# Attention of a decoder layer: a new order of query tiles, and VectorE's counts placed between single operations

## The reference, cut to what matters

```
dots  = einsum('bqhd,bsd->bqhs', qi, kidx) * IDX_DIM ** -0.5      # 8 indexer heads of 64
score = einsum('bqhs,bqh->bqs', relu(dots), wi)
score = where(kpos <= qpos, score, -inf)
idx   = top_k(score, 256)
s     = q . k[idx] * HEAD_DIM ** -0.5                              # 8 heads, 4 K/V heads
o     = softmax(s) @ v[idx]
```

## Time and profile before

| | us |
|---|---|
| median of 3 runs | 3550.71 (3544.14 to 3551.95) |
| the profiled execution | 3548.39 |
| its span | 3546.6 |
| outside the span | 1.8 |
| attention phase, of the span | 925.6 to 2008.6 |

### The profile page before, as it was taken

One profiled execution on the slowest core, in us unless ns is written; L12 is line 12 of the kernel. 1 busy time (PEld: TensorE's weight loads), 2 busy tenths in 40 slices (PEclk: granted clock), 3 DMA queues, 4 the chain that ended last, 5 costly groups with the idle time before them and its releaser, 6 DMA issues. The chain is left out here.

```text
span 3546.6 us, 45686 instructions
## 1 busy us (share of the span) xinstructions
PE 2941.8 (83%) x15200; PEld 1827.0 (52%) x15201; DVE 1971.5 (56%) x2856; ACT 1053.8 (30%) x1832; POOL 837.6 (24%) x1259
## 2 busy tenths in 40 slices
PE   7999999998666566666667686999999499999989
PEld 6877899988523333333445453445444333333333
DVE  2697025990267777778876367743323543444437
ACT  1111121211266675758585441000000011111113
POOL 2344333322253342414030131012120000000013
PEclk9999999999767887887879897999999599999989
DMA  3323222434100000000000265223331378677537
GB/s 120 97 92 122 90 71 75 142 120 131 46 19 13 15 13 10 10 10 7 7 7 10 81 209 185 84 101 126 118 128 39 143 274 299 261 286 286 185 132 241
DMA packets 218484, 390.29 MB, mean 110 GB/s; under 512 B 28180, under 2 KB 147220, under 8 KB 205514
## 3 DMA queue, kind: packets, MB, share of 16 engines
q1 hardware_dynamic: 184818, 268.60, 22.3%
q0 software_dynamic: 25152, 89.03, 7.5%
q10 hardware_dynamic: 8352, 30.51, 2.2%
HBM read 501.30 MB, written 88.52 MB: 166 GB/s over the span
## 5 line engine op out<-in xcount | busy, mean ns | idle before, releaser
L347 PE MATMUL p_ps_acc<-p_x_hi,p_w_hi 128*128 128x352 f32 (+2 forms) x1480 | 525.1, 355 | 26.0 <-POOL p_w_lo L284 22.3
L347 PE MATMUL p_ps_acc<-p_x_lo,p_w_hi 128*128 128x352 f32 (+2 forms) x1480 | 524.3, 354 | 0.0
L347 PE MATMUL p_ps_acc<-p_x_hi,p_w_lo 128*128 128x352 f32 (+2 forms) x1480 | 523.9, 354 | 0.0
L832 PE MATMUL q_ps_s<-a_keys,q_q_st 64*128 64x512 f32 (+3 forms) x640 | 196.5, 736 | 237.8 <-ACT q_relu L914 132.4
L532 DVE SCALAR_TENSOR_TENSOR p_conv<-p_uh,p_taps,p_conv 128x1024 f32<-128x1024 f32 x240 | 384.2, 1601 | 8.5
L2457 PE MATMUL e_ps_G<-l_wgu,e_xT 128*64 x768 | 341.8, 598 | 21.3 <-DVE e_gu_b L2574 10.8
L2459 PE MATMUL e_ps_G<-e_gu_b,e_xT 128*64 128x512 f32 x768 | 341.9, 599 | 0.0
L347 PEld LDWEIGHTS p_ps_acc<-p_x_hi,p_w_hi 128*128 128x128 f32 (+1 forms) x1480 | 277.8, 188 | 55.9 <-POOL p_w_lo L284 22.8
L347 PEld LDWEIGHTS p_ps_acc<-p_x_lo,p_w_hi 128*128 128x128 f32 (+1 forms) x1480 | 279.0, 189 | 28.5
L1016 DVE TENSOR_SCALAR_CACHE_REDUCE q_junk_dve<-q_sc,q_mid 128x384 bf16<-128x384 f32 (+6 forms) x175 | 247.0, 1411 | 82.0 <-POOL q_mid L1129 79.9
L347 PEld LDWEIGHTS p_ps_acc<-p_x_hi,p_w_lo 128*128 128x128 f32 (+1 forms) x1480 | 277.9, 188 | 27.3
(11 more groups left out here) (406 smaller groups left out, 4858.4 us busy)
## 6 DMA issues: line engine op xcount, KB each, us to landing
l_wgu<-in_w_gate_dram SPq DMA_DIRECT2D x96, 1024.0 KB
l_wgu<-in_w_up_dram SPq DMA_DIRECT2D x96, 1024.0 KB
l_wd<-in_w_down_dram SPq DMA_DIRECT2D x96, 1024.0 KB
p_w<-in_w_in_dram SPq DMA_DIRECT2D x72, 512.0 KB, 3.8
yb<-e_y SPq DMA_DIRECT2D x48, 512.0 KB, 4.6
x_gates<-featT SPq DMA_DIRECT2D x64, 256.0 KB
featT<-p_stage ACTq DMA_DIRECT2D x28, 528.0 KB
featT<-p_stage ACTq DMA_DIRECT2D x28, 512.0 KB
```

What stands on the lines that cost most here:

```text
L347: m = nc.tensor.matmul(acc[slot][tb][0:rows, 0:width], wp[:, slot, k, 0:rows], xp[:, k, at], start=(k == 0 and i == 0), stop=(k == KD - 1 ...
L832: m = nc.tensor.matmul(ps_s[x][:, k0:k1], q_st[rows, t % 2, g % 4, :], kT[rows, g % 4 // 2, a + k0:a + k1], start=True, stop=True)
```

## The change

There are two edits. The first is a table `TILES` that says which tile is done at which position: positions 0 to 15 hold tiles 0, 1, 4, 5, 10, 11, 14, 15, 12, 13, 8, 9, 6, 7, 2, 3. Everything that depended on the tile's number as a length, a row of the inputs and outputs, or the end of an accumulation now goes through `TILES`; buffers, semaphores and slots go by position as before. In blocks of keys, the three jobs of each cycle are:

| cycle | attention before | search before | dots before | attention after | search after | dots after |
|---|---|---|---|---|---|---|
| 0 | 1, 2 | 3, 4 | 5, 6 | 1, 2 | 5, 6 | 11, 12 |
| 1 | 3, 4 | 5, 6 | 7, 8 | 5, 6 | 11, 12 | 15, 16 |
| 2 | 5, 6 | 7, 8 | 9, 10 | 11, 12 | 15, 16 | 13, 14 |
| 3 | 7, 8 | 9, 10 | 11, 12 | 15, 16 | 13, 14 | 9, 10 |
| 4 | 9, 10 | 11, 12 | 13, 14 | 13, 14 | 9, 10 | 7, 8 |
| 5 | 11, 12 | 13, 14 | 15, 16 | 9, 10 | 7, 8 | 3, 4 |
| 6 | 13, 14 | 15, 16 | - | 7, 8 | 3, 4 | - |
| 7 | 15, 16 | - | - | 3, 4 | - | - |

The prologue makes the dots of 5 and 6 blocks instead of 3 and 4.

The second edit is in VectorE's order. The two operations of the first half's `sums` are taken apart: head 0, place 2, head 1, place 3, then `normalise` where it is due, place 4.

```diff
+TILES = [0, 1, 4, 5, 10, 11, 14, 15, 12, 13, 8, 9, 6, 7, 2, 3]
+
 def length(t):
-    return (t + 1) * P
+    return blocks(t) * P
+
+def blocks(t):
+    return TILES[t] + 1
+
+def rows_at(t):
+    return slice(TILES[t] * P, TILES[t] * P + P)
...
-                sp.dma_start(qi_st[:, t % 2], c.featT[COL_QI:COL_KI, t * P:(t + 1) * P]...
+                sp.dma_start(qi_st[:, t % 2], c.featT[COL_QI:COL_KI, rows_at(t)]...
...
-                    for k in range(t + 1):
+                    for k in range(blocks(t)):
...
-                def sums(t, m, half):
+                def sums(t, m, half, heads=(0, 1)):
...
-                    for x in range(2):
-                        src, w = relu[:, n % 2, x, 0:b - a], wi_tok[:, t, 2 * m + x:2 * m + x + 1]
+                    for x in heads:
+                        src, w = relu[:, n % 2, x, 0:b - a], wi_tok[:, TILES[t], 2 * m + x:2 * m + x + 1]
...
                     behind(g, 1)
-                    if dotted_in(g):
-                        sums(dotted_in(g), g % 4, 0)
+                    if here:
+                        sums(here, g % 4, 0, (0,))
                     behind(g, 2)
+                    if here:
+                        sums(here, g % 4, 0, (1,))
+                    behind(g, 3)
                     if g % 4 == 0 and t:
                         normalise(t - 1)
-                    behind(g, 3)
                     behind(g, 4)
```

More of the change, by code:

```diff
@@ L674, in __init__ @@
             for x in range(2):
-                for a, b in cuts(t + 1, 4):
+                for a, b in cuts(blocks(t), 4):
                     self.turns[g, x, a // 4] = turn
@@ L712, in last_turn @@
     def last_turn(self, g, x):
-        return self.turns[g, x, g // 4 // 4]
+        return self.turns[g, x, TILES[g // 4] // 4]
 def attend_prompt(nc, c, kT, kiT, v_tok, wi_tok):
@@ L876, in values @@
                             m = nc.tensor.matmul(ps_o[x * HD:(x + 1) * HD, g % 4, :], v_tok[:, k, kv * HD:(kv + 1) * HD], pT[:, x, k, :],
-                                                 start=(k == 0), stop=(k == t))
-                            if k == t:
+                                                 start=(k == 0), stop=(k == TILES[t]))
+                            if k == TILES[t]:
                                 m.then_inc(pv_done, 1)
@@ L919, in keep_turned @@
                         act.wait_ge(pv_done, 2 * g)
-                    for a, b in cuts(g // 4 + 1, 4):
+                    for a, b in cuts(blocks(g // 4), 4):
                         n = at.turns[g, x, a // 4]
@@ L1010, in bracket @@
                     ch.link(nc.vector.tensor_reduce(least[:, t:t + 1], row, AX.X, ALU.min))
-                    ch.link(nc.vector.tensor_tensor(row[:, t * P:], row[:, t * P:], mk[:, P:2 * P], ALU.add))
+                    ch.link(nc.vector.tensor_tensor(row[:, length(t) - P:], row[:, length(t) - P:], mk[:, P:2 * P], ALU.add))
                     nc.vector.tensor_reduce(most[:, t:t + 1], row, AX.X, ALU.max).then_inc(range_ready, 1)
@@ L1049, in behind, with masked @@
                         choose(t + 1, n - HALVINGS - 5)
-                def masked(g, u):
+                def masked(g, u, heads=(0, 1)):
                     t = g // 4
+                    if u >= len(cuts(length(t), 1024)):
+                        return
                     a, b = cuts(length(t), 1024)[u]
@@ L1092, in _ @@
                     t, nxt = g // 4, (g + 1) // 4
-                    if g and dotted_in(g - 1):
-                        sums(dotted_in(g - 1), (g - 1) % 4, 1)
+                    last, here = (dotted_in(g - 1) if g else None), dotted_in(g)
+                    if last:
+                        sums(last, (g - 1) % 4, 1)
                         if g % 4 == 0:
-                            bracket(dotted_in(g - 1))
+                            bracket(last)
                     if g + 1 < NSLOT:
```

9 lines of the change are left out of this document (4 added, 5 removed).

## The result

The changed kernel runs in 3502.61 us (median of 4 runs, 3500.33 to 3504.78), against 3550.53 us for the kernel before (3544.14 to 3551.95). The ratio is 0.9874, with a 95% interval of 0.9861 to 0.9888.

The account below looks back on a forecast made before the run. No engine is near full over the span; VectorE's idle time, cycle by cycle in the attention phase, was to decide. Prologue +5, loop work -5, idle -8 and split -7 gave -15 us: 3536 us, range 3504 to 3566.

Parts of the forecast that it names:

- Cycle 7: Last cycle, attention of 3 and 4 blocks: 39 us in all, VectorE idle 26 us instead of 66.6, a gain of 40.
- Part 3, the idle time by cycle: VectorE's idle time over the attention phase's eight cycles: 276 us instead of 284, 8 us less.
- Cycle 3: Longest attention beside search and dots: 1.6 us a slot more than old cycle 5, so VectorE idle 48 us.
- the ring: Long cycles' chain of relu freeing a bank, TensorE's scores, VectorE's mask and ScalarE's copies; longer scores and transposes lengthen it.
- the paragraph on the clock: TensorE's clock: a denser middle would run cycle 3 at full clock and the last cycle slow; the forecast did not use it.
- Part 4, the split: VectorE's count put between the two heads' sums: 7 us less, at most 27, at least nothing.
- Part 1, the prologue: Dots before the loop, now of 5 and 6 blocks: about 3.4 us a pair of heads, loop starts 5 us later.
- Part 2, the work: VectorE's work in the loop: from 767 to 762 us, 5 us less, as dots of four blocks move to the prologue.
- signs of being wrong: In the profile after: cycle 3 over 208 us, cycles 2 and 3 each under 32 idle, or middle waits unchanged in number.
- The split pays in full: Rival: the count between the sums gains its whole bound of 27 us, 20 more than forecast, 3516 us; chance 0.17.
- Slower, by the ring of cycle 3: Rival: TensorE stays at the low clock in cycle 3, 3.8 us a slot, 30 over the cycle, 3566 us; chance 0.15.
- Idle time is a constant of 28 us a cycle: Rival: VectorE's idle time is 7 x 28.4 + 26 = 225 us, 59 less than 284, kernel 3485 us; chance 0.10.

Follow-up runs that it names:

- e2: The changed kernel with VectorE's old order, both heads' sums in one place, so the new tile order alone; 3503.86 us, ratio 0.9875 to the kernel before.
- e3: The new-tile-order-only kernel with another table: tiles 0, 1, 4, 5, 6 and on to 15 rising, then 2, 3; 3516.44 us.
- e8: The changed kernel with places 1 and 2 both before the first half's sums, which are joined again; 3490.96 us.
- e1: The changed kernel with the tiles in the old order 0 to 15, so VectorE's changed order alone; 3545.41 us, ratio 0.9992 to the kernel before.
- e6: The changed kernel with the first half's sums replaced by passes with one on-chip input, still split; 3491.24 us.
- e7: The new-tile-order-only kernel with the first half's sums replaced by passes with one on-chip input, heads joined, without the split; 3502.88 us.
- e5: The changed kernel with place 4 moved over the slot's end, between the two heads' sums of the second half; 3515.18 us.

## Why the prediction was wrong, point by point

**The sign and the mechanism of the order: right.** Cycle 7 gives back most, and the cycles that take over the long tiles lose a part. e2 and e3 show both.

**Part 3, the idle time by cycle: the step that failed.** For the order alone I had 276 us; e2 measured 244.3 by its windows. The forecast let cycle 7 give back 40 us and the cycles that take over the long tiles lose 32 of them. In e2 cycle 7 gives back 47.1 us (66.6 less 19.5), and the seven others together lose 7.4 (217.4 to 224.8). Term by term, forecast and measured in e2:

| cycle | forecast | order only | difference |
|---|---|---|---|
| 0 | 39 | 34.0 | -5.0 |
| 1 | 29 | 26.2 | -2.8 |
| 2 | 35 | 30.9 | -4.1 |
| 3 | 48 | 37.6 | -10.4 |
| 4 | 34 | 41.1 | +7.1 |
| 5 | 35 | 30.0 | -5.0 |
| 6 | 30 | 25.0 | -5.0 |
| 7 | 26 | 19.5 | -6.5 |

- *Cycle 7.* I took 4.3 us a slot and a tail of 9 us, neither from a row. A slot of the changed kernel, TensorE alone:

```profile
1935.37 0.92 PE L844 MATMUL q_ps_s<-a_keys,q_q_st 64*128 64x384 f32 x4
1936.22 0.87 PE L861 MATMUL q_ps_t<-g_ident,q_sm 128*128 128x128 f32 x6
1937.77 0.88 PE L888 MATMUL q_ps_o<-q_pT,a_keys 128*64 128x128 f32 x12 [0.68 <-ACT q_pT L935]
1938.58 1.13 PE L844 MATMUL q_ps_s<-a_keys,q_q_st 64*128 64x512 f32 x4
```

  From one group of scores to the next it is 3.21 us here; the slots of the 3-block tile take 3.2 to 3.4 us and those of the 4-block tile up to 4.05. Seven slots are 25 us instead of 30, and 6.5 us follow instead of 9. The granted clock is 1.00 (windows above), though TensorE is busy for 25.0 of 31.5 us only. No gap of TensorE in this cycle is over 0.84 us, so the rule of the Trainium skill that the clock drops after the array has stood idle ("TensorE: Matmul & The Clock Gate", Part 1) is not contradicted; what I had made of it in the forecast, a slow last cycle, did not come.
- *Cycle 3.* I added 1.0 us for longer scores and 0.5 for transposes, and something for the low clock, to every slot, as if all lay in the ring. Over the old cycle 5 (35.2) it was 2.4 us in the whole cycle, not 13. The granted clock was 0.85, against 0.82 in the old cycle 5; so it went the way that I had weighed in the paragraph on the clock and not used, but not to the full clock that I had put there. How much is the clock and how much is cover by VectorE's other work no run here takes apart.
- *Cycle 4.* The one term that was too low. I likened it to the old cycle 6, which has no dots, and gave the relu 7 us. In the changed kernel it waits there as long as in the old cycles 4 and 5 with their long dots (21.5 and 15.3 us):

```profile
DVE q_sc L1015 <- ACT q_relu L926: 16.2, 6, 5.9
```

  This is 16.2 us, and L1013 adds 4.3. My reading, which no run isolates, is that the ring from mask over scores, transposes and dots to the relu goes by the length of the attention, and that the place 1 that covers it now holds a short count. e8 gave it a second cover and took 3 us off cycle 4 and 6.7 off cycle 5.
- *Cycles 0, 1, 2, 5 and 6* were each taken 3 to 5 us too high, all the same way, so the errors added up to 22 us. I had taken the upper part of each analogy.

**Part 4, the split: the size was wrong, by a mechanism that I had not named.** Forecast -7, bound -27; in the phase it was -1.8 beside the new order and -3.4 alone. I wrote that the sum of head 1 "covers the middle's way round". It covers hardly any of it, since GpSimd stands still beside it: the count behind it still waits 0.80 us on average, against the 0.92 of the earlier trace rows, which e1's timeline and e6 against e7 explain. The sign I had for the bound (an edit that can only help) came out by chance: e5, another spread of the counts, cost 12.6 us by the medians.

**Part 1, the prologue.** Forecast +5, measured 30.2 us against 29.0, +1.2. The period of 3.4 us held for the first five pairs of heads (3.2 to 3.4) and not for the last three (2.3). An early pair and a late one:

```profile
931.64 2.50 PE L829 MATMUL q_ps_s<-a_keys,q_qi_st 64*128 64x512 f32 x8 [0.72 <-ACT q_relu L926]
...
943.91 1.56 PE L829 MATMUL q_ps_s<-a_keys,q_qi_st 64*128 64x512 f32 x8 [0.78 <-ACT q_relu L926]
```

The granted clock, the third number from the end in these windows, was 0.51 up to 941.5 us and 1.00 from there to 949.2:

```profile
925.20:941.50 16.30, 12.94 (x40) 6.00 (x40) 7.79 (x10) 6.20 (x10) 0.00 (x0) 0.51 0.19 49
941.50:949.20 7.70, 4.71 (x26) 2.13 (x26) 6.55 (x9) 5.21 (x9) 1.75 (x3) 1.00 0.02 4
```

TensorE had done groups of 2.5 us with gaps of 0.7 to 0.9 us before it rose. In the kernel before, with groups of 1.65 to 2.08 us and gaps of 0.9 to 1.2 us, it was 0.50 throughout. So from the first dots to the first scores it is 24.0 us, as before (23.8), instead of the 27.4 of the forecast (eight times 3.4 is 27.2). The forecast had left the clock out of this part. **Part 2, the work** fell by 7.6 us, and by 4.9 us with the order alone (762.2 us in e2), as forecast; the other 2.7 came with the split.

**The rivals.** Of the forecast's own signs of being wrong, one came in full: the waits for the middle are unchanged in number (89 against 91). "The split pays in full" is refuted by e1. "Slower, by the ring of cycle 3" did not come: cycle 3 took 183.4 us. "Idle time is a constant of 28 us a cycle" (3485 us) had 0.10 and came nearest in its mechanism: the first seven cycles of the changed kernel have 32.3 us on average, with cycles 3 and 4 above 38, and the time lies two thirds of the way from the forecast to that case. The range was too narrow below because I let it go only partway there, and its end isn't worked out: halfway from the forecast to 3485 is 3510, halfway from the full split is 3500, and 3504 is neither.

## What to carry to other kernels

In a software pipeline whose work items differ in size, look at the ends before the middle: the last stage runs alone, so the smallest item belongs there; e3 shows that this one step brings 31 of 44 us. Before an operation is put between two others to cover a third engine's latency, look up in the trace what that third engine does beside this kind of operation: a cover that holds up what it covers is worth next to nothing. And where VectorE's own result comes back to it through GpSimd only to be compared and added on one column, two short operations on VectorE can be faster than the way round: they cost 81 us of busy time here, took away waits of 107.8 us, and the phase fell by 14.2.

## What the runs showed of the hardware

- GpSimd's one-column operations take 0.30 and 0.38 us beside a VectorE pass with one on-chip input and a running sum. Beside one that reads two tensors, those that are held end 0.08 to 0.26 us after the pass does, so they take up to 1.46 us. Where the first half's passes are of the first kind, 18 of 684 such operations take over 0.6 us; in the changed kernel, 56.
- A plain `tensor_scalar` with one on-chip tensor (0.75 us for 1024 columns) holds them too: 0.73 us instead of 0.30.
- TensorE's granted clock was 1.00 with 25.0 us busy of 31.5 in short groups, with gaps of at most 0.84 us. In the prologue it rose from 0.51 to 1.00 when the groups were of 2.5 us, and stayed at 0.50 in the kernel before with groups of 1.65 to 2.08 us.
- On VectorE, an operation on one column cost 211 to 273 ns of busy time, in a chain where each waits for the one before.
